# Attention front of a hybrid decoder step: the prompt compression swaps its operands and moves under the projection, the block selection moves into the attention loop, and the first cached keys are turned ahead of that loop

## The reference, cut to what matters

```python
proj = h @ w_in                                  # q, three pairs of k and v, gates
ck, cv = _compress(k_cmp, ...), _compress(v_cmp, ...)   # einsum('bnlgd,lde->bnge'): blocks of 32 rows
s = jnp.einsum('bqgrd,bngd->bqgrn', qg, ck) * scale     # compressed branch
p_c = _masked_softmax(s, vis); o_c = einsum(p_c, cv)
imp = sum of p_c over the heads of a group, per 64-row block
_, idx = lax.top_k(score, n_sel)                 # the selected blocks
o_s, o_w = attention over the selected blocks, over the window
o = g[..., 0:1] * o_c + g[..., 1:2] * o_s + g[..., 2:3] * o_w
```

## Time and profile before

| | |
|---|---|
| median of 3 runs | 2287.47 us (2285.99 to 2290.71) |
| profiled execution | 2286.44 us, its span 2284.6 us |
| PE busy | 2035.1 us, 89% of the span |
| DVE, ACT busy | 1529.8 us, 1178.2 us |
| projection starts | 290.65 us into the span |
| prompt loop starts, ends | 480.86 us, 583.02 us |
| output weights' matmuls start | 714.67 us |

### The profile page before, as it was taken

One profiled execution on the slowest core, in us unless ns is written; L12 is line 12 of the kernel. 1 busy time (PEld: TensorE's weight loads), 2 busy tenths in 40 slices (PEclk: granted clock), 3 DMA queues, 4 the chain that ended last, 5 costly groups with the idle time before them and its releaser, 6 DMA issues.

```text
span 2284.6 us, 31300 instructions
## 1 busy us (share of the span) xinstructions
PE 2035.1 (89%) x10715; PEld 1611.5 (71%) x10715; DVE 1529.8 (67%) x2051; ACT 1178.2 (52%) x1333; POOL 14.9 (1%) x26
## 2 busy tenths in 40 slices
PE   5888899869747899997977999999999999999994
PEld 3555543735535799997965878888888878788883
DVE  6656510267522544445567989898989989898984
ACT  3545400124310333333226778777778877777771
POOL 0000000100000000000000000000000000000000
PEclk9999999557978999998987999999999999999996
DMA  9788722200357665443415999999999999999970
GB/s 280 258 285 291 258 74 69 77 0 1 117 168 197 242 210 166 165 166 110 141 56 206 360 349 341 347 346 348 352 347 353 361 337 345 355 340 345 344 286 23
DMA packets 262794, 537.68 MB, mean 235 GB/s; under 512 B 14876, under 2 KB 56068, under 8 KB 262438
## 3 DMA queue, kind: packets, MB, share of 16 engines
q1 hardware_dynamic: 258514, 520.34, 65.1%
q0 software_dynamic: 1984, 13.45, 1.7%
q10 hardware_dynamic: 2196, 2.61, 0.4%
HBM read 533.32 MB, written 11.35 MB: 238 GB/s over the span
## 4 chain that ended last, share of the span: by engine, by line
PE 77%; DVE 7%; SPq 5%; issue 4%; ACT 2%; DMA 2%; POOL 0%; DVEq 0%; ACTq 0%; PEldq 0%; POOLq 0%
PE ps L1478 14%; PE ps L2023 13%; PE ps L1988 8%; PE ps L1990 8%; PE ps L1989 8%; PE ps L1829 5%; PE ps L1831 5%; PE ps L1830 5%; SPq L520 2%; SPq L521 2%; PE ps L1936 1%; DVE alo L874 1%; PE ps L1709 1%; DMA ring<-in_w_ada 1%; PE ps L1972 1%
## 5 line engine op out<-in xcount | busy, mean ns | idle before, releaser
L1420 DVE TENSOR_TENSOR wlo<-ring,whi 128x1024 fp32r<-128x1024 f32 x672 | 796.9, 1220 | 84.6 <-ACT whi L825 59.1
L825 ACT ACTIVATE whi<-ring 128x1024 fp32r<-128x1024 f32 x672 | 706.7, 1061 | 211.3 <-PE ps L1990 131.1
L1988 PE MATMUL ps<-whi,XTh 128*128 128x512 f32 x896 | 355.3, 397 | 4.4 <-DVE wlo L1420 4.4
L1990 PE MATMUL ps<-whi,XTl 128*128 128x512 f32 x896 | 350.6, 391 | 0.0
L1989 PE MATMUL ps<-wlo,XTh 128*128 128x512 f32 x896 | 350.3, 391 | 0.0
L1988 PEld LDWEIGHTS ps<-whi,XTh 128*128 128x128 f32 x896 | 168.8, 188 | 37.5 <-issue 4.8
L1990 PEld LDWEIGHTS ps<-whi,XTl 128*128 128x128 f32 x896 | 168.7, 188 | 36.6
L1989 PEld LDWEIGHTS ps<-wlo,XTh 128*128 128x128 f32 x896 | 169.0, 189 | 32.1
L1239 DVE TENSOR_TENSOR flo<-ring,fhi 128x2048 fp32r<-128x2048 f32 x42 | 96.2, 2291 | 138.0 <-ACT fhi L633 138.0
L633 ACT ACTIVATE fhi<-ring 128x2048 fp32r<-128x2048 f32 x42 | 80.4, 1914 | 174.7 <-PE ps L1831 174.7
L874 DVE TENSOR_TENSOR alo<-ring,ahi 128x2048 fp32r<-128x2048 f32 x48 | 109.4, 2281 | 76.8 <-ACT ahi L626 76.7
(11 more groups left out here) (332 smaller groups left out, 3141.8 us busy)
## 6 DMA issues: line engine op xcount, KB each, us to landing
ring<-in_w_moe_gu SPq DMA_DIRECT2D x224, 1024.0 KB, 6.6
ring<-in_w_moe_down SPq DMA_DIRECT2D x112, 1024.0 KB, 7.0
ring<-in_w_ada SPq DMA_DIRECT2D x48, 1024.0 KB, 8.3
ring<-in_w_ff_gu SPq DMA_DIRECT2D x28, 1024.0 KB, 5.4
ring<-in_cache_cmp_kv SPq DMA_DIRECT2D x128, 128.0 KB, 4.2
ring<-in_cache_sel_kv SPq DMA_DIRECT2D x128, 128.0 KB, 2.1
ring<-in_w_ff_down SPq DMA_DIRECT2D x14, 1024.0 KB, 5.1
ring<-in_w_conv_in SPq DMA_DIRECT2D x12, 1024.0 KB, 5.1
```

What stands on the lines that cost most here:

```text
L825: a.activation(whi[:, i % SPLIT, c0:c0 + HALF], ring[:, (T_MOE + i) % RING, c0:c0 + HALF], ACT.Copy).then_inc(s_split_hi, 1)
L1420: v.tensor_tensor(wlo[:, i % SPLIT, c0:c0 + HALF], ring[:, (T_MOE + i) % RING, c0:c0 + HALF], whi[:, i % SPLIT, c0:c0 + HALF].bitcast(F32) ...
L1988: pe.matmul(out, XTh[:, kc, :], hi, start=kc == 0, stop=False)
L1990: ins = pe.matmul(out, XTl[:, kc, :], hi, start=False, stop=kc == 7)
```

## The change

Projection and compression: PE projects four tiles, turns the four raw groups of cache rows (columns 1024 to 1535 of `proj`), projects the gates, then the fifth tile. The compression follows at once and no longer waits for `s_kv_stored`. It holds 16 columns of tokens as the stationary operand and moves the 128 columns of `wbd` past them. Its output lies the other way round (`crow`), so that a copy and two small transposes are added. DVE rotates q already behind the second tile. The turning of q and k comes behind the compression. `s_kv_stored` is now waited for ahead of the first cached keys, whose destination overlies `proj`.

Softmax and selection: the compressed softmax is done for both halves of the prompt at once. The selection is cut into 12 pieces, `select(0)` to `select(11)`, that DVE does at the end of the loop's first 12 steps.

Cached keys: the keys of pair 0 (12 groups of 4 transposes) are turned ahead of the prompt's loop and evicted by ACT alone (`take_key0`). Behind the loop the scores of pair 0 come at once.

```diff
-            for ct in range(6):
-                n = T_NSA + 2 * ct
+            def project(ct):
+                n = T_NSA + 2 * ct + (ct == 4)
...
-            pe.wait_ge(s_qk_prompt, 16)
-            pe.wait_ge(s_qk_sample, 12)
-            pe.wait_ge(s_kv_stored, 1)
+            for ct in range(4):
+                project(ct)
+            pe.wait_ge(s_ck_ready, 1)
+            pe.wait_ge(s_proj_dve, 3)
+            pe.wait_ge(s_proj_act, 3)
+            for i, c0 in enumerate((1024, 1152, 1280, 1408)):
+                if i >= 2:
+                    pe.wait_ge(s_raw_taken, i - 1)
+                for t in range(2):
+                    ins = pe.transpose(ps[:, 6 + i % 2, 128 * t:128 * t + 128], proj[:, t, c0:c0 + 128], ident)
+                ins.then_inc(s_raw_turned, 1)
...
+            project(4)
+
+            pe.wait_ge(s_raw_taken, 4)
             for kv in range(2):
                 src = Ttail[:, kv, :].rearrange("p (n l) -> p n l", l=32)
                 for l in range(32):
-                    ins = mm(ps[:, 4, 16 * kv:16 * kv + 16], wbd[:, kv, l, :], src[:, :, l], l, 32)
+                    ins = mm(ps[0:16, 6, 128 * kv:128 * kv + 128], src[:, :, l], wbd[:, kv, l, :], l, 32)
             ins.then_inc(s_pcmp_done, 1)
...
+            pe.wait_ge(s_kv_stored, 1)
+            for g in range(12):
+                i, q = g // 4, g % 4
+                if q == 0:
+                    wait_tile(pe, tile_k[0] + i)
+                if g >= 3:
+                    pe.wait_ge(s_key0_taken, g - 2)
+                for j in range(4):
+                    page, gp = (4 * (q % 2) + j, q // 2) if i < 2 else (4 * (q // 2) + j, q % 2)
+                    ins = pe.transpose(ps[:, 4 + g % 3, 128 * j:128 * j + 128],
+                                       pages(tile_k[0] + i)[:, page, 128 * gp:128 * gp + 128], ident)
+                ins.then_inc(s_key0_turned, 1)
...
+            pe.wait_ge(s_key0_taken, 12)
+            pe.wait_ge(s_cprob_ready, 1)
...
+                if 5 <= i < 9:
+                    t = i - 5
+                    si_ = score[:, t].unsqueeze(1).to_broadcast([128, 17, 17])
+                    sj_ = score[:, t].unsqueeze(2).to_broadcast([128, 17, 17])
+                    v.tensor_tensor(rank[:, 0, t], si_, sj_, ALU.is_gt)
+                    link(v.tensor_tensor(rank[:, 1, t], si_, sj_, ALU.is_equal))
+                    link(v.tensor_tensor(rank[:, 1, t], rank[:, 1, t], C("before").rearrange("p (j i) -> p j i", j=17), ALU.mult))
+                if i == 9:
+                    link(v.tensor_tensor(rf[0], rf[0], rf[1], ALU.add))
+                if i == 10:
+                    link(v.tensor_reduce(sn, rf[0], AX, ALU.add))
...
-            turn_keys(0)
```

More of the change, by code:

```diff
@@ L418, in trunk @@
         T_NSA = len(stream)
-        for ct in range(5):
+        for ct in range(4):
             pair(A["w_nsa_in"][0], ct * 512)
         stream.append([(0, 128, quarter(A["w_nsa_in"][0], 0, 2560, 8, 48), 8)])
+        pair(A["w_nsa_in"][0], 4 * 512)
         T_SEL = len(stream)
@@ L710, in _ @@
+            for i in range(12):
                 a.wait_ge(s_qk_turned, i + 1)
[L711 to L718, removed]
+                dst = qT[:, i, :] if i < 8 else kTp[:, (i - 8) % 2, (i - 8) // 2, :]
+                a.activation(dst, ps[:, i % 6, 0:SEQ], ACT.Copy).then_inc(s_qk_prompt, 1)
@@ new lines, in take_keys @@
+            def take_keys(tau):
+                j = j_keys(tau)
+                for b2 in range(2):
+                    if tau >= 2:
+                        a.wait_ge(s_seq_scores, 2 * (tau - 2) + b2 + 1)
+                    for q in range(4):
+                        if (j + 4 * b2 + q) % 2 == 0:
+                            take(j + 4 * b2 + q, TS[:, tau % 2, b2, q // 2, 512 * (q % 2):512 * (q % 2) + 512])
+                for q in range(4):
+                    if (j + 8 + q) % 2 == 0:
+                        take(j + 8 + q, TW[:, tau % 2, q // 2, q % 2, :])
@@ new lines, in take_key0 @@
+            def take_key0(g):
+                a.wait_ge(s_key0_turned, g + 1)
+                i, q = g // 4, g % 4
+                dst = TS[:, 0, i, q // 2, 512 * (q % 2):512 * (q % 2) + 512] if i < 2 else TW[:, 0, q // 2, q % 2, :]
+                a.activation(dst, ps[:, 4 + g % 3, :], ACT.Copy).then_inc(s_key0_taken, 1)
+            a.wait_ge(s_cscore_shift, 1)
+            a.activation(ScP, ScP, ACT.Exp, scale=SCALE).then_inc(s_cscore_exp, 1)
+            for g in range(3):
+                take_key0(g)
@@ L1043, in _ @@
                     v.wait_ge(s_rope_done, 3 * grp + t + 1)
+            project(0)
+            project(1)
+            rope(0, 2)
+            for ct in range(2, 5):
+                project(ct)
+            rope(1, 5)
             v.wait_ge(s_gate_exp, 3)
@@ new lines, in _, with turn_keys @@
+            ins.then_inc(s_cscore_done, 1)
+            def turn_keys(tau):
+                for i in range(3):
+                    n = tile_k[tau] + i
+                    wait_tile(pe, n)
+                    for q in range(4):
+                        bk = bank_free()
+                        for j in range(4):
+                            page, gp = (4 * (q % 2) + j, q // 2) if i < 2 else (4 * (q // 2) + j, q % 2)
+                            ins = pe.transpose(ps[:, bk, 128 * j:128 * j + 128],
+                                               pages(n)[:, page, 128 * gp:128 * gp + 128], ident)
+                        ins.then_inc(s_bank_turned, 1)
+                    pe.wait_ge(s_bank_turned, jb[0])
+                    pe.sem_inc(s_pe_read, 1)
```

272 lines of the change are left out of this document (139 added, 133 removed).

## The result

The changed kernel took 2236.57 us in the median of 4 runs (2233.46 to 2238.80), the kernel before 2288.49 in 4 runs beside it: a ratio of 0.9772 with the interval 0.9756 to 0.9789. The forecast was 2235 with a range of 2223 to 2249. In a later comparison the same kernel gave 2238.27 and a ratio of 0.9786 (0.9773 to 0.9799), so 49 to 52 us are gained.

The account below looks back on a forecast made before the run. TensorE was taken to set the time, SP's queue the tail. Gains of 37 (front), 0 (loop) and 15.8 (tail), 52.8 us, take 2286.44 to 2233.6; the median lies 1.03 above: 2235 us, range 2223 to 2249.

Parts of the forecast that it names:

- Up to the compression: Ahead of the loop: fifth tile ends at 403.4 us, then the compression takes 15.7 us at clock 1.00.
- lower bound of 13.7: Compression: 13.7 us, half of the old 27.46, if only the clock helps.
- Turning and small matmuls: Behind the compression: turning q and k 6.4 us, small matmuls 5.6 us, plus 1 us for a falling clock.
- First keys and loop start: Ahead of the loop: key evictions by ACT 10 us, probabilities 1.4; loop starts at 443.9, 37 us gained.
- ACT waiting for PE among the keys: Sign of being wrong, at the first keys ahead of the loop, where ACT's evictions were expected back to back.
- The loop: 0: Attention loop: gain of the first four steps set against 1 to 2 us of selection; 0, bounds -9 and +3.
- bound of -9: Attention loop: at most 9 us gained, if the clock holds.
- the clock holds into the loop: Rival: the clock stays up, the loop gives 9 us and the small matmuls 1; 2225 us, chance 0.20.
- The tail: 15.8: Behind the loop: SP's queue starts 3.3 us later but with one 19.1 us group fewer; 15.8 us gained.
- just fits: Tail: v0's release comes 24 us behind the scores, and SP needs it 25 us behind them.
- SP pausing ahead of v1: Sign of being wrong, in the tail: SP's queue stops before the v1 fetch.
- tail gives nothing: Rival: SP stands for v0's release or PE's last pair sets the end; 2251 us, chance 0.08.

Follow-up runs that it names:

- old_operands: The changed kernel with the compression in its old operand form (128 x 128 weights stationary, 16 columns moved), in its new place; 2249.43 us, ratio 0.9843.
- swap_alone: The kernel before with only the compression's operands swapped (raw columns as weights, compression weights moving), place and order unchanged; 2274.87 us, ratio 0.9945.
- warm_fill: The changed kernel with seven extra matmuls of no use in the attention loop's fill; 2236.17 us, ratio 0.9777.
- select_early: The changed kernel with the whole selection put back ahead of the attention loop; 2245.00 us, ratio 0.9823.
- key0_late: The changed kernel with the first pair's keys turned behind the loop again, by ScalarE and VectorE in turns; 2249.59 us, ratio 0.9839.
- warm_steps: The changed kernel with extra matmuls in the loop's fill and one more in each further step of its first half; 2221.13 us, ratio 0.9712.
- after_again: The changed kernel itself run once more, beside its variants; 2238.27 us, ratio 0.9786 to the kernel before.

## Why the prediction was right

**Up to the compression.** Its end of the fifth tile, 403.4, is the measured 403.41. The compression was put at 15.7 us by the duration of transposes and took 14.13, 0.110 a record; I had taken 0.123. old_operands shows 0.108 for the old form at full clock, so both forms are near the lower bound of 13.7 (0.107 a record), which I had derived for the clock alone. That the form was needed to hold the clock, which the step took for granted, is shown from both sides by swap_alone and old_operands.

**Turning and small matmuls.** 6.4 forecast, 6.6 to the last transpose (424.1), though 1.0 of the 6.4 was meant for what follows it: a group of three transposes took 0.56 us where I had 0.45. The clock fell at the compressed scores, as forecast, but these then took nearly their old 7.00 us (6.78), so the 1 us for it was too little: 9.5 us from 424.1 to 433.58 where I had 6.6. The compression had ended 1.9 us early, so 1.2 us of this are left, and the next step gives them back.

**First keys and loop start.** 10 us bounded by ScalarE, then 1.4: measured 433.58 to 443.65, 10.07 with both in it. The first 4 of these were not ScalarE's: PE's first 16 transposes ran low, in 3.75 us. The sign of being wrong, "ACT waiting for PE among the keys", shows only as two gaps of 0.34 and 0.21 us. The loop start was forecast at 443.9 and came at 443.65; the 37 us are right in sum, by misses of up to 3 us that cancelled: to that exactness it is luck.

Behind those 16 transposes the clock is up, once more (3.75, then 1.97 us). Not all transposes do that: the 36 of q and k in old_operands, 10.37 us without a gap, ran at 0.50 to their end, and so did the 44 of the kernel before, 12.29 us. The prediction had this row and let transposes bring the clock up all the same. What sets the two kinds apart isn't shown.
The Trainium skill (TensorE: Matmul & The Clock Gate, Part 4) has transposes not count as busy; by it the next 32 key transposes would have run low too. There the trace disagrees, as it did before; the 36 and the 44 of q and k agree with it.

**The loop: 0.** Right (0.3 lost), with the reason partly wrong: the clock fell in the fill, before any selection, at 447.6. In warm_fill, with the fill filled, it fell in step 7, among the selection's steps, as forecast; that the selection is the reason isn't shown, since no run had a filled fill and no selection in the loop. The 1 to 2 us that were to come through are about 1, by select_early beside key0_late, and the start at 1.00 gave back some 0.5 of it. The bound of -9 for a clock that holds was close: warm_steps gained 11.2. I had named the rival "the clock holds into the loop" with 2225; it measured 2221, but the program doesn't get there without help.

**The tail: 15.8.** This is the mis-sized term: 11.3 in the first trace, 14.9 in the second. The step said that v0's release "just fits", 24 us behind the scores against the 25 at which SP needs it. In the first trace it came at 27.2 and SP needed it at 23.7, so SP stood for 4.4 us, which was the prediction's own sign of being wrong ("SP pausing ahead of v1"). The step took PE's turning and transposing from a stretch in which they ran at full clock, on PE before the change:

```profile
598.59 1.97 PE L1724 MATMUL ps<-con,ring 128*128 128x128 f32 x16 [2.85 <-DVE work L879]
600.86 1.97 PE L1724 MATMUL ps<-con,ring 128*128 128x128 f32 x16 [0.30 <-PE ps L1724]
606.54 1.70 PE L1768 MATMUL ps<-con,attn 128*128 128x128 f32 x12 [3.71 <-DVE attn L1210]
```

In the changed kernel the same three took 3.65, 2.97 and 2.82 us, 3.8 more together. Of the 4.5 us missing from the 15.8, some 3 are SP's standing. Another 2 lie at the end: the output weights' matmuls began 17.0 us after SP had reached them, 2 more than before; in after_again it was 15.1, and why isn't shown. The direction of the rival "tail gives nothing" was right, its size small.

**Sum.** 52.8 forecast; 47.6 in spans for the first trace, 50.1 for the second (2234.5), 49 to 52 in the medians.

## What to carry to other kernels

Before narrowing or moving work, ask of each stretch which form of it leaves the clock up: the same 128 records took 14 or 25 us by which operand moved, and one matmul per step that nobody needs gained 15 us. Better still, put needed work of the next stage (here key transposes) into those waits: it raised the clock, and it freed blocks, which took a group of fetches, 19 us, out of the tail. A release that "just fits" should be costed at the low clock too.

## What the runs showed of the hardware that was not expected

A TensorE that is busy without a gap can still lose its clock: 104 records of 128 x 128 weights with 16 moved columns, PE busy 21.80 of 21.80 us, all at 0.50 (old_operands), and 64 records with 8 columns at 0.53 over 6.80 us in the changed kernel. 16 key transposes at 0.50 were followed by 32 at 1.00, while the 36 transposes of q and k in old_operands ran at 0.50 for 10.37 us. Adding matmuls to a loop that TensorE bounded made it 11.2 us shorter, because all of them ran at 1.00 (warm_steps). Executions of one kernel differ in where the clock falls: the tail of the same program took 120.4 and 116.8 us.
